# Sums of x for an FFN's first pair of column blocks in three groups, and another order of work in its first two pairs

## What is computed

```
def rms_norm(x, g):
    xf = x.astype(jnp.float32)
    y = xf * lax.rsqrt(jnp.mean(xf * xf, axis=-1, keepdims=True) + EPS)
    return (y * g.astype(jnp.float32)).astype(x.dtype)

def swiglu(x, w_gu, w_down):
    gu = x @ w_gu
    return (jax.nn.silu(gu[..., :D_FF]) * gu[..., D_FF:]) @ w_down

...
    for l in range(DEPTH):
        x = x + 0.5 * swiglu(rms_norm(x, p['ffn1_norm'][l]), p['ffn1_w_gu'][l], p['ffn1_w_down'][l])
        hn = rms_norm(x, p['mix_norm'][l])
...
        x = x + y
        x = x + 0.5 * swiglu(rms_norm(x, p['ffn2_norm'][l]), p['ffn2_w_gu'][l], p['ffn2_w_down'][l])
```

## Time and profile before

| | us |
|---|---|
| three runs | 2045.15, 2042.05, 2044.31 |
| median | 2044.31 |
| the profiled execution | 2043.77 |
| its span, first to last instruction | 2042.0 |
| TensorE busy | 1959.9 (96%) |
| VectorE busy | 1505.9 (74%) |
| ScalarE busy | 964.0 (47%) |

### The profile page before, as it was taken

The page is one execution under the profiler, slowest core; times in us unless marked ns, Lnnn a source line. Parts: engine busy times, 40 slices in busy tenths (PEclk is TensorE's granted clock), DMA queues, the critical chain, the costliest instruction groups (busy, mean ns, idle before and its releaser), DMA issues.

```text
span 2042.0 us, 34956 instructions
## 1 busy us (share of the span) xinstructions
PE 1959.9 (96%) x14465; PEld 1933.5 (95%) x14465; DVE 1505.9 (74%) x2111; ACT 964.0 (47%) x1490; POOL 58.1 (3%) x82
## 2 busy tenths in 40 slices
PE   4999999999998999999979999999999999999996
PEld 4999999999998999999979999999988999999996
DVE  5966957788778858758689578587575787586676
ACT  5543534437755525425465245254365554253352
POOL 0000000002200000000000000000010000000001
PEclk9999999999999999999989999999999999999998
DMA  3231222222221322322222223223200122222221
GB/s 134 84 104 64 103 88 99 79 90 81 83 86 62 110 77 83 104 83 79 81 74 103 84 83 107 80 83 123 83 32 1 63 84 104 82 93 94 83 88 62
DMA packets 55151, 172.69 MB, mean 85 GB/s; under 512 B 6320, under 2 KB 12752, under 8 KB 54976
## 3 DMA queue, kind: packets, MB, share of 16 engines
q1 hardware_dynamic: 53200, 166.09, 23.4%
q0 software_dynamic: 784, 3.04, 0.4%
q10 hardware_dynamic: 1008, 1.31, 0.2%
HBM read 167.72 MB, written 3.69 MB: 84 GB/s over the span
## 4 chain that ended last, share of the span: by engine, by line
PE 87%; DVE 7%; ACT 3%; issue 2%; DMA 1%; DVEq 0%; SPq 0%; ACTq 0%
PE ps L564 46%; PE ps L535 37%; PE ps L758 1%; PE ps L783 1%; DVE rstd L1431 1%; DMA raw<-w_gu 1%; DVE xs_lo L1266 1%; PE ps L768 1%; DVE gw L1266 1%; PE ps L639 0%; ACT xs_hi L1013 0%; PE ps L863 0%; DVE gw_f L1501 0%; DVE raw L1296 0%; DVE x L1753 0%
## 5 line engine op out<-in xcount | busy, mean ns | idle before, releaser
L564 PE MATMUL ps<-xs_hi,gw 128*128 128x288 f32 x4928 | 1004.8, 297 | 55.7 <-DVE gw L1266 23.7
L564 PEld LDWEIGHTS ps<-xs_hi,gw 128*128 128x128 f32 x4928 | 801.9, 190 | 61.2 <-DVE gw L1266 24.3
L564 PE MATMUL ps<-xs_lo,gw 128*128 128x288 f32 x2464 | 731.8, 297 | 0.0
L564 PEld LDWEIGHTS ps<-xs_lo,gw 128*128 128x128 f32 x2464 | 467.3, 190 | 0.2
L1266 DVE TENSOR_TENSOR gw<-raw,gw 128x1024 fp32r<-128x1024 f32 x352 | 383.2, 1091 | 83.1 <-ACT gw L923 33.4
L535 PE MATMUL ps<-act_hi,w_hi 128*128 128x288 f32 x1632 | 349.4, 296 | 0.4 <-DVE w_lo L1266 0.4
L535 PE MATMUL ps<-act_lo,w_hi 128*128 128x288 f32 x1632 | 349.5, 296 | 0.0
L535 PE MATMUL ps<-act_hi,w_lo 128*128 128x288 f32 x1632 | 349.3, 296 | 0.0
L901 ACT ACTIVATE w_hi<-raw 128x1024 fp32r<-128x1024 f32 (+1 forms) x142 | 143.5, 1010 | 366.9 <-PE ps L535 361.4
L535 PEld LDWEIGHTS ps<-act_hi,w_hi 128*128 128x128 f32 x1632 | 262.8, 189 | 0.6 <-issue 0.6
L535 PEld LDWEIGHTS ps<-act_lo,w_hi 128*128 128x128 f32 x1632 | 263.0, 189 | 0.0
(11 more groups left out here) (204 smaller groups left out, 1964.5 us busy)
## 6 DMA issues: line engine op xcount, KB each, us to landing
raw<-w_gu SPq DMA_DIRECT2D x176, 512.0 KB, 4.0
raw<-w_dn SPq DMA_DIRECT2D x32, 512.0 KB, 3.6
raw<-w_dn SPq DMA_DIRECT2D x32, 384.0 KB, 3.3
raw<-w_dn SPq DMA_DIRECT2D x32, 320.0 KB, 3.1
raw<-w_rec SPq DMA_DIRECT2D x20, 512.0 KB, 3.3
raw<-w_dn SPq DMA_DIRECT2D x32, 192.0 KB, 2.4
raw<-w_out SPq DMA_DIRECT2D x8, 512.0 KB, 3.3
raw<-w_q SPq DMA_DIRECT2D x8, 512.0 KB, 3.3
```

The lines of the kernel that those rows point to most:

```text
L564: ins = nc.tensor.matmul(ps[:, bank, 0:HT], gv(wt, w)[:, 0, p * P:(p + 1) * P], xb(xt, p, b)[:, 0, :], start=start and i == n == 0, stop=s ...
```

## The change

Three things are edited.

The sums of x come in three groups. The block order becomes B11, T1, B21, B22, T3, T2, T4. Group one (B11, T1) needs only the lower tile of a pair, group two is B21, B22, group three T3, T2, T4. Each group has its own rounding on ScalarE and its own low half on VectorE (two of 576 columns and one of 864, where there were one of 864 and one of 1152), and `cmb_ready` counts three to a tile pair.

`first_pair` no longer goes tile by tile in the second to fourth FFN: P1 of all four tiles, P2 of three, P5 of four, P2 of the last. The statistics move behind P6, in all four FFNs.

ScalarE and VectorE get `first_windows` for the first two pairs of an FFN. The root comes behind V1 of pair 0, and the SiLU of pair 0 behind V1 of pair 1. On VectorE the gate's sum is parted from its scaling; the reciprocal (in the third FFN the copy of the V tile, `keep_values`) stands between the two, behind the second up half of pair 0.

The blocks of x and TensorE's program:

```diff
-B11, B21, B22, T1, T3, T2, T4 = range(X_BLOCKS)
+B11, T1, B21, B22, T3, T2, T4 = range(X_BLOCKS)
...
-            def p637(g):
+            def p637(g, stat=None):
                 a = bank_a(g)
                 pe.wait_ge(snap1_made, g + 1)
                 product(a, X2, T2, False, stop=False).then_inc(p6_done, 1)
+                if stat is not None:
+                    stats(stat)
...
+                tiles = list(enumerate(PORDER[f]))
+                if f == 0:
+                    for i, p in tiles:
+                        ins1, ins2, ins5 = p1(i, p), p2(i, p), p5(i, p)
+                else:
+                    for t in tiles:
+                        ins1 = p1(*t)
+                    for t in tiles[:3]:
+                        p2(*t)
+                    for t in tiles:
+                        ins5 = p5(*t)
+                    ins2 = p2(*tiles[3])
...
-                if stat is not None:
-                    stats(stat)
-                p637(g)
+                pe.wait_ge(cmb_ready, 12 * f + 12)
+                p637(g, stat)
```

ScalarE's first two windows, and its part of `mixer_out`:

```diff
+            def first_windows(g, stat):
+
+                hi_x43(g)
+                snap_1(g)
+                hi_a22(g)
+                hi_a(g + 1)
+
+                act.wait_ge(cmb_ready, 12 * (g // FT) + 12)
+                snap_5(g)
+                snap_v1(g)
+                if stat is not None:
+                    root(stat)
+                hi_x12(g + 1)
+
+                snap_v2(g)
+                hi_x43(g + 1)
+                snap_1(g + 1)
+                hi_a22(g + 1)
+                hi_a(g + 2)
+                snap_5(g + 1)
+                snap_v1(g + 1)
+                silu(g)
+                hid_hi(g, 0, 0)
+                hi_x12(g + 2)
...
                 for m in range(KD):
                     prep_next(j0 + m)
-                    if m == 5:
-                        hi_a(FT * f)
-                    if m == 6:
-                        hi_x12(FT * f)
...
                     x_scaled_to(f, i, x_temp, m % 2)
-                    if m % 2:
+                    if m % 2 == 0:
+                        square(m, stat)
                         x_hi_first(f, i)
-                    square(m, stat)
-                    if m % 2:
+                    else:
+                        x_hi_second(f, i)
+                        square(m, stat)
                         x_hi_rest(f, i)
+                    if m == 4:
+                        hi_a(FT * f)
+                    if m == 6:
+                        hi_x12(FT * f)
```

VectorE's first two windows, the sums of x, and its part of `mixer_out`:

```diff
-            def gate_out_of(g):
+            def gate_sum(g):
...
                 nc.vector.tensor_tensor(two(y), ps[:, b:b + 2, 0:HT], two(s12), ALU.add).then_inc(y_sum_made, 1)
+
+            def gate_scaled(g):
                 dve.wait_ge(y_sum_made, g + 1)
                 nc.vector.tensor_tensor(y, y, rstd[:, :], ALU.mult).then_inc(y_scaled, 1)
...
+            def first_windows(g, stat):
+
+                lo_x43(g)
+                lo_a22(g)
+                sum_x14(g + 1)
+                lo_a(g + 1)
+                sum_x23(g + 1)
+                lo_x12(g + 1)
+
+                gate_sum(g)
+                lo_x43(g + 1)
+                up_second(g)
+                if stat is not None:
+                    invert(stat)
+                else:
+                    keep_values()
+                gate_scaled(g)
+                lo_a(g + 2)
+                hidden(g)
+                lo_a22(g + 1)
+                sum_x14(g + 2)
+                hid_lo(g, 0)
+                sum_x23(g + 2)
+                lo_x12(g + 2)
...
+            def x_t1(f, i):
+
+                t = X_TEMPS[f][i]
+                dve.wait_ge(xg_made, 2 * (N_PAIR * f + i) + 1)
+                nc.vector.tensor_tensor(t[:, T1, :], t[:, B11, :], t[:, B12, :], ALU.subtract).then_inc(cmb_t1, 1)
...
             def x_sums(f, i):
 
                 t = X_TEMPS[f][i]
                 dve.wait_ge(xg_made, 2 * (N_PAIR * f + i + 1))
-                own(nc.vector.tensor_tensor(t[:, T1:T3 + 1, :], t[:, B11:B22 + 1:2, :],
-                                            t[:, B12:B12 + 1, :].broadcast_to([P, 2, HT]), ALU.subtract))
-                own(nc.vector.scalar_tensor_tensor(t[:, T2, :], t[:, B22, :], -1.0, t[:, T1, :],
-                                                   ALU.mult, ALU.subtract))
+                dve.wait_ge(cmb_t1, N_PAIR * f + i + 1)
+                t2 = mark(nc.vector.scalar_tensor_tensor(t[:, T2, :], t[:, B22, :], -1.0, t[:, T1, :],
+                                                         ALU.mult, ALU.subtract))
+                nc.vector.tensor_tensor(t[:, T3, :], t[:, B22, :], t[:, B12, :], ALU.subtract)
+                dve.wait_ge(dve_chain, t2)
                 nc.vector.scalar_tensor_tensor(t[:, T4, :], t[:, T2, :], -1.0, t[:, B21, :],
                                                ALU.mult, ALU.subtract).then_inc(cmb_sums, 1)
 
-            def x_lo(f, i):
+            def x_lo(f, i, part):
...
+                first, n = ((B11, 2), (B21, 2), (T3, 3))[part]
+                dve.wait_ge(cmb_hi, 3 * (N_PAIR * f + i) + part + 1)
+                sub(xb(xs_lo, p, first, n), t[:, first:first + n, :], xb(xs_hi, p, first, n).bitcast(F32), cmb_ready)
...
                     prep_next(j)
-                    if m % 2:
-                        x_sums(f, m // 2)
-                        x_lo(f, m // 2)
                     if m == 6:
                         sum_x23(g)
+                    if m % 2 == 0:
+                        x_t1(f, m // 2)
+                        x_lo(f, m // 2, 0)
+                    else:
+                        x_sums(f, m // 2)
+                        x_lo(f, m // 2, 1)
+                        x_lo(f, m // 2, 2)
+                    if m == 5:
+                        lo_a(g)
+                    if m == 6:
                         lo_x12(g)
                     add_square(m, stat)
-                    if m == 5:
+                    if m == 4:
                         sum_x14(g)
-                        lo_a(g)
```

More of the change, by code:

```diff
@@ L590, in first_pair, with p1, p2, p5 @@
                     pe.wait_ge(dve_evac, evac(c0 - 2))
-                for i, p in enumerate(PORDER[f]):
-                    pe.wait_ge(cmb_ready, 8 * f + 2 * i + 1)
-                    ins1 = product(a, A11, B11, i == 0, (p,), False)
-                    ins2 = product(a + 1, A12, B21, i == 0, (p,), i == 3)
+                def p1(i, p):
+                    pe.wait_ge(cmb_ready, 12 * f + 3 * i + 1)
+                    return product(a, A11, B11, i == 0, (p,), False)
+                def p2(i, p):
+                    pe.wait_ge(cmb_ready, 12 * f + 3 * i + 2)
+                    return product(a + 1, A12, B21, i == 0, (p,), i == 3)
+                def p5(i, p):
                     if i == 0:
@@ L955, in window, with snap_5, snap_v1 @@
                 nc.scalar.activation(s1, ps[:, bank_a(g), 0:HT], ACT.Copy).then_inc(snap1_made, 1)
[L956 to L957 removed]
+            def snap_5(g):
+                act.wait_ge(p5_done, g + 1)
+                if g:
+                    act.wait_ge(c22_made, g)
+                nc.scalar.activation(s5, ps[:, bank_a(g) + 2, 0:HT], ACT.Copy).then_inc(snap5_made, 1)
+            def snap_v1(g):
+                act.wait_ge(p6_done, g + 1)
+                nc.scalar.activation(s2, ps[:, bank_a(g), 0:HT], ACT.Copy).then_inc(snapv1_made, 1)
+            def window(g, g0, g1, c0):
+                if g > g0:
+                    snap_v2(g - 1)
+                hi_x43(g)
+                snap_1(g)
                 if g > g0:
@@ L980, in ffn @@
                     g0, g1, c0 = pairs_of(f, c)
-                    for g in range(g0, g1):
-                        window(g, g0, g1, c0, stat_in if c == 0 and g == g0 else None)
+                    if c == 0:
+                        first_windows(g0, stat_in)
+                    for g in range(g0 + 2 * (c == 0), g1):
+                        window(g, g0, g1, c0)
                     snap_v2(g1 - 1)
@@ L1361, in ffn @@
                     g0, g1, c0 = pairs_of(f, c)
-                    for g in range(g0, g1):
+                    if c == 0:
+                        first_windows(g0, stat_in)
+                    for g in range(g0 + 2 * (c == 0), g1):
                         window(g, g0, g1, c0)
-                        if c == 0 and g == g0 and stat_in is not None:
-                            invert(stat_in)
-                        if f == 2 and c == 0 and g == g0 + 1:
-                            keep_values()
-                    gate_out_of(g1 - 1)
+                    gate_sum(g1 - 1)
+                    gate_scaled(g1 - 1)
                     up_second(g1 - 1)
```

74 lines of the change are left out of this document (38 added, 36 removed).

## The result

| | before | changed |
|---|---|---|
| median, us | 2043.40 (19 runs) | 2046.35 (19 runs) |
| range, us | 2040.59 to 2045.15 | 2043.93 to 2048.72 |
| profiled execution, its span, us | 2043.77, 2042.0 | 2048.5, 2046.6 |

The ratio is 1.0017, with a 95% interval of 1.001 to 1.0024: 0.17% slower (the medians alone, 2.95 us apart, make 0.14%). That is inside the 0.2% that counts as no change here, though the interval leaves no room for a gain. The forecast was 2046.8. The profiled execution of the changed kernel, 2048.5, lies 2.15 us above its median; all that is read from its trace has to be seen with that.

What follows compares the result with a forecast made beforehand. TensorE was taken as busy nearly throughout, so only its idle stretches could be won. Terms -3.2 - 3.2 + 2.2 + 7.2 = +3.0 on the profiled 2043.77 gave 2046.8 us, own range 2044 to 2049.

Steps and rivals of the forecast that it cites:

- The V2 stop: Every FFN, pair 1: product 4 waits for ScalarE's V2 snapshot behind the X1/X2 rounding; costs 3.35 us, clock fall 1.4 behind.
- The rival without a fall: Every FFN: no clock fall after the new V2 stop, 1.4 us less four times, 2041.2; chance 0.10.
- the one without a wait: Every FFN: V2 snapshot there in time, 3.35 and 1.4 us less, four times, 2027.8; chance 0.08.
- The reciprocal hidden: VectorE, first pairs: the scaling after it ends some 2 us before SiLU could start, so its 3.75 us are hidden.
- Product 6 in the second and fourth FFN: Pair 0: product 6 waits for the s1 snapshot behind the last x group; the stop costs 1.1 us.
- the last residual tile comes no earlier: Rival, second and fourth FFN: last residual tile not added earlier, 1.1 us more twice, 2049.0; chance 0.06.
- The gain of 3.2 in these two: Second and fourth FFN: five stops worth 7.66 us go, new ones of 1.1 and 3.35 come; 3.2 gained each.
- The first FFN: Product 6 waits uncovered for s1, then 32 statistics rows at 0.23 us; loss 2.2 us in all.
- the rival of the longer low clock: First and third FFN: low clock lasts one stretch longer, 1.5 us each, 2049.8; chance 0.18.
- The third FFN: Product 6 comes 2.4 us later by TensorE's new order, plus new stop 3.35 and clock fall 1.4; loss 7.2 us.
- VectorE's path there: Third FFN: VectorE's work about equal; the skill page's instruction cost would add 1.25 us for eight more instructions, total 2048.0.
- The table load: Rival, ScalarE: table switch costs more in its new place, 1.38 us more in each of four chains, 2052.3; chance 0.03.

Runs made afterwards that it cites:

- e1: Changed kernel with the V2 snapshot of pair 1 issued on ScalarE ahead of the rounding of X1 and X2 of pair 2: 2038.04 us, 0.9976 of the kernel before.
- e11: Changed kernel with the first pair going tile by tile in all four FFNs: 2042.39 us, 0.9994 of the kernel before.
- e2: Changed kernel with the first pair going tile by tile again in the third FFN alone: 2042.44 us, 0.9996 of the kernel before.
- e3: Changed kernel with the 32 statistics matmuls ahead of product 6 again in the first FFN: 2039.39 us, 0.9980 of the kernel before.
- e8: Changed kernel with the first FFN's s1 snapshot of pair 0 taken after three of the eight squares: 2041.81 us, 0.9989 of the kernel before.
- e7: Only the x groups in three parts, windows and statistics as in the kernel before, third FFN's first pair tile by tile: 2034.33 us, 0.9957 of the kernel before.
- e5: Changed kernel with pair 1's V2 snapshot early, third FFN tile by tile, first FFN's statistics ahead of product 6: 2029.47 us, 0.9927 of the kernel before.

## Why the prediction was right, and where its terms were off

- **The V2 stop**: right. 0.27 and 2.56 us of idle with 0.26 for each make 3.35, as forecast, within 0.01 in all four FFNs; e1 shows the cause by taking it away. The clock fell behind each of the four. The rival without a fall and the one without a wait are out in this execution; among the experiments that keep this stop, e11 shows it once without a fall, in its first FFN.
- **The reciprocal hidden**: the 1.18 us in which VectorE waits for the SiLU, after the reciprocal and the scaling, bear it out. The third FFN has no reciprocal there and the same stop (2.57 us at 1076.33). No run took the reciprocal away.
- **Product 6 in the second and fourth FFN**: 0.86 and 1.01 us, with 0.26 about the 1.1 forecast. That the last residual tile comes no earlier is out as well.
- **The gain of 3.2 in these two**: 3.70 and 3.60. Which of the five removed stops was worth 0.4 more than its row was not tried.
- **The first FFN** is the term that came out too small: loss 3.22, forecast 2.2. The step that failed is the 32 statistics rows at 0.23, 7.4 us. Product 6 came at 38.16 (37.8) and ended at 41.18 (40.7) as described, but the clock stayed low to 43.09, so the statistics took 8.47 and product 3 came at 49.65, not 48.5. This is the rival of the longer low clock, in this FFN alone. It is also partly a matter of the execution: in the same code product 3 came at 48.28 in e2, where the clock rose at 40.6 and the statistics took 7.55, at 49.18 in e1 and at 49.97 in e11. e3 and e8 (43.9 and 43.4) show that 4.4 to 6.6 us behind it hang on one snapshot's place.
- **The third FFN** is the term that was too large: forecast 7.2. The stage lost 6.32, but it begins with a wait of VectorE for weights, and that ended at the same time in both kernels, though the second FFN was 0.44 late. Counted from there, as the forecast did, the loss is 6.75. VectorE's timeline, before and changed:

```profile
1023.09 1.23 DVE L1296 TENSOR_TENSOR raw<-raw 128x1024 f32<-128x1024 f32 x1 [3.80 <-DMA raw<-w_gu]
...
1023.10 1.23 DVE L1363 TENSOR_TENSOR raw<-raw 128x1024 f32<-128x1024 f32 x1 [3.42 <-DMA raw<-w_gu]
```

  Of the 27 matmuls behind 1049.18 not 24 but 17 ran at half clock, since it rose at 1053.4; product 6 came near 1054.8, where 1055.1 was forecast. The order itself was sized about right: 2.4 forecast, 2.6 to 2.7 by e2, e7 and e11 with the clock counted equal.
- **VectorE's path there**: the last pair's low halves took 2.39 us in three pieces from 1048.38, where two took 2.32 from 1048.26, so from the same start at 1023.1 the path ended 0.19 us later with eight more instructions. The estimate of 1.25 us, by the cost between instructions that the Trainium skill states (VectorE: DVE Perf Modes, the section on the TRN2 errata), is out. VectorE's timeline of the changed kernel:

```profile
1048.38 2.39 DVE L1333 TENSOR_TENSOR xs_lo<-act_lo_f,xs_hi 128x576 fp32r<-128x576 f32 x3
```

- **The table load**: 1.28 us, and the SiLU follows 0.02 us later, so that rival is out too.

The sum of 3.0 met 2.95 in the medians. Five stops gone, the late V2 snapshot with its clock fall in all four FFNs, the exposed wait for s1 in the first and the burst that comes too late in the third are all where the prediction had them. In the traces its four terms make 2.24 where 3.0 was forecast: +1.0 in the first FFN and -0.9 in the third nearly cancel, -0.9 is in the second and fourth. The trace's total, 4.7 us, holds 2.44 of falls in code that no term covers, of which the medians hold less. So the mechanism was right, and that the sum met the medians within 0.1 is in part luck.

## What to carry to other kernels

Where engines work through fixed orders, moving one wait away makes the next instruction in that order the late one: before a move, list what then stands ahead of each snapshot that TensorE needs, and put those that depend on nothing but TensorE ahead of those that wait for a third engine. Judge a stop by the granted clock behind it as well as by its own length: here shortening one from 2.6 to 1.5 us was worth twice the difference. Time the parts of a change apart: by the medians these two hid 6.3 us won under 9.3 us lost.

## What was not expected of the hardware

The same stop is followed by a clock fall in one execution and not in the next. Over the fourteen profiled executions (before, changed, twelve experiments): the stops of 2.55 to 2.57 us in the FFNs were followed by one in 26 of 29 places, those of 1.53 to 1.55 us (e1, e5) in none of 8. A stop of 2.42 us in the recurrent layer, which no edit touches, was followed by one in 8 of 14, one of 1.79 us at the second FFN's end in 2 of 14, one of 1.25 us in the attention in 1 of 14. TensorE's timeline of the changed kernel has these two stops right ahead of the two low stretches in the layers:

```profile
554.46 0.55 PE L536 MATMUL ps<-xs_hi,w_hi 128*128 128x300 f32 x2 [2.42 <-ACT gw_f L1162]
...
1505.83 1.90 PE L778 MATMUL ps<-keep,gw_f 64*128 64x128 f32 x8 [1.25 <-ACT gw_f L1236]
```

Each fall costs 0.9 to 1.6 us by the ledger, as much as several edits here; for that reason traces were compared stage by stage. What decides between the two outcomes was not settled, and the length of the stop alone does not: near 32 us in the first FFN, where TensorE waits for x tiles shortly after the clock has risen, stops of 1.60 to 1.94 us were followed by a fall within 0.9 us in all six executions that have them. How long the clock then stayed low varies as well: in the same code of the first FFN 10.2 us in the changed kernel and e1, 6.8 in e2 and e11.
